# A hybrid encoder layer on eight cores: a convolution tap moved to VectorE, another order of tokens in PSUM, first norms and last block cut differently

## What is computed

```python
x = x + 0.5 * swiglu(rmsnorm(x, norm_ffn1[l]), w_ffn1_in[l], w_ffn1_out[l])
h = rmsnorm(x, norm_mix[l])
aq, ak, av, mq, mk, mv, mo, mif, cq, gts = jnp.split(h @ w_in[l], split_pts, axis=-1)
# mixer A: 24 heads of 64, groups (window, dilation) = (128,1), (512,4), (2048,16)
aq = rope(rmsnorm(ah(aq), att_q_gain[l])) * (ATT_HEAD_DIM ** -0.5)
ak = rope(rmsnorm(ah(ak), att_k_gain[l]))
y_att = dilated_attention(aq, ak, ah(av)).astype(x.dtype)
# mixer B: bidirectional mLSTM, behind a centred depthwise convolution of width 5
mqk = jax.nn.silu(centred_dwconv(jnp.concatenate([mq, mk], axis=-1), ml_conv_w[l], ml_conv_b[l]))
...
# mixer C: cross-attention of 4 heads into 256 memory tokens
...
merged = (g[:, :, 0] * (y_att @ w_br_att[l]) + g[:, :, 1] * (y_ml @ w_br_ml[l])
          + g[:, :, 2] * (y_cx @ w_br_cx[l]))
x = x + merged @ w_out[l]
x = x + 0.5 * swiglu(rmsnorm(x, norm_ffn2[l]), w_ffn2_in[l], w_ffn2_out[l])
x = rmsnorm(x, norm_final[l])
```

## Time and profile before

| | |
|---|---|
| runs shown (us) | 3948.44, 4095.29, 4669.13; median 4095.29 |
| profiled execution | 3949.09 us |
| its span on the slowest core (core 6) | 3947.6 us; the eight cores 3931.2 to 3947.6 |
| granted TensorE clock, mean of the cores | 0.992 to 0.995 |
| TensorE matmul, weight load | 97%, 49% of the span; 23860 matmuls |
| VectorE, ScalarE, GpSimd | 44%, 37%, 26% |
| DMA, mean | 67 GB/s |

### The profile page before, as it was taken

How to read it: one execution, slowest core, us unless ns; L and a number is a source line. 1 busy time by engine, 2 the same in 40 slices (tenths; PEclk the granted TensorE clock), 3 DMA queues, 4 the chain that set the end, 5 groups by cost and what they waited for, 6 DMA issues and landing times.

```text
span 3947.6 us, 64651 instructions; the slowest of 8 cores (3931.2 to 3947.6 us)
## 1 busy us (share of the span) xinstructions
PE 3811.1 (97%) x23860; PEld 1932.7 (49%) x23860; DVE 1755.9 (44%) x2559; ACT 1444.7 (37%) x2389; POOL 1035.8 (26%) x1048
## 2 busy tenths in 40 slices
PE   6999999998999999999989999999889999999998
PEld 2444457644555444444434444666455544444443
DVE  3121425656884444121441214357578744432214
ACT  4101233477775222101331012345778842321012
POOL 3010124346771012000221002144367601110002
PEclk9999999999999999999999999999999999999999
DMA  6152332343345433222444213225233433332212
GB/s 139 23 80 32 90 65 52 76 87 67 61 87 100 76 71 50 40 36 39 111 109 58 38 26 107 54 55 108 55 71 72 101 70 76 70 51 39 38 23 89
DMA packets 252882, 265.74 MB, mean 67 GB/s; under 512 B 161440, under 2 KB 179104, under 8 KB 250272
## 3 DMA queue, kind: packets, MB, share of 16 engines
q0 software_dynamic: 65088, 127.04, 21.8%
q1 hardware_dynamic: 187488, 134.58, 12.6%
HBM read 318.31 MB, written 57.67 MB: 95 GB/s over the span
## 4 chain that ended last, share of the span: by engine, by line
PE 91%; DVE 3%; ACT 2%; issue 2%; POOL 1%; DMA 1%; SPq 0%; DVEq 0%; POOLq 0%; ACTq 0%
PE ps L467 91%; DVE arena L467 3%; ACT arena L467 2%; POOL arena L467 1%; DMA arena<-arena 0%; ACT L467 0%; SPq L467 0%; DMA arena<-x 0%; DMA arena<-scr_y 0%; DMA scr_y<-arena 0%; DVEq L466 0%; POOLq L484 0%; ACTq L466 0%; DVEq L484 0%; POOLq L466 0%
## 5 line engine op out<-in xcount | busy, mean ns | idle before, releaser
L467 PE MATMUL ps<-arena 128*128 128x512 bf16 (+5 forms) x23860 | 3811.1, 321 | 126.2 <-DVE arena L467 50.8
L467 PEld LDWEIGHTS ps<-arena 128*128 128x128 bf16 x23860 | 1932.7, 99 | 2004.4 <-issue 228.3
L467 ACT ACTIVATE arena<-ps 128x512 bf16<-128x512 f32 (+7 forms) x1346 | 820.3, 638 | 1745.1 <-PE ps L467 1722.4
L467 DVE TENSOR_TENSOR arena<-ps,arena 128x512 f32<-128x512 f32 (+4 forms) x936 | 714.3, 776 | 1486.4 <-PE ps L467 1403.1
L467 POOL TENSOR_TENSOR arena<-arena 128x512 f32<-128x512 bf16 (+4 forms) x592 | 792.4, 1352 | 802.1 <-DVE arena L467 375.4
L467 DVE SCALAR_TENSOR_TENSOR arena<-ps,arena 128x512 f32<-128x512 f32 (+2 forms) x488 | 343.3, 710 | 401.2 <-PE ps L467 352.3
L467 ACT ACTIVATE arena<-arena 128x512 f32<-128x512 f32 (+3 forms) x654 | 387.2, 608 | 288.8 <-DVE arena L467 259.5
L467 DVE TENSOR_TENSOR arena<-arena 128x512 bf16<-128x512 f32 (+5 forms) x428 | 341.0, 805 | 60.0 <-ACT arena L467 40.2
L467 ACT ACTIVATE arena<-ps,arena 128x512 f32<-128x512 f32 (+3 forms) x320 | 204.3, 657 | 389.2 <-PE ps L467 365.7
L467 DVE SCALAR_TENSOR_TENSOR arena<-arena 128x512 bf16<-128x512 f32 (+2 forms) x296 | 233.1, 853 | 70.7 <-ACT arena L467 66.0
L467 POOL DMA_DIRECT2D arena<-wst x120 | 68.0, 567 | 521.1 <-PE ps L467 520.4
(11 more groups left out here) (16 smaller groups left out, 32.3 us busy)
## 6 DMA issues: line engine op xcount, KB each, us to landing
arena<-wst POOLq DMA_DIRECT2D x120, 256.0 KB, 4.2
arena<-w1a POOLq DMA_DIRECT2D x88, 256.0 KB, 4.9
arena<-w2a POOLq DMA_DIRECT2D x88, 256.0 KB, 4.5
arena<-x SPq DMA_DIRECT2D x32, 512.0 KB, 7.7
scr_x<-arena SPq DMA_DIRECT2D x8, 2048.0 KB, 9.2
arena<-scr_x SPq DMA_DIRECT2D x32, 512.0 KB, 9.4
out<-arena SPq DMA_DIRECT2D x32, 512.0 KB, 2.8
scr_v<-arena SPq DMA_DIRECT2D x48, 256.0 KB, 3.0
```

Of the source, the lines that this page charges most:

```text
L467: ins = getattr(eng, rec.name)(**rec.kwargs)
```

## The change

Six edits in one:

1. `conv` leaves its fifth tap to DVE: four matmuls, then one multiply-add on DVE which reads the bank and `cb` and writes a float32 tile (`cvr`), from which SiLU reads. The diagonal matrices have four parts.
2. In the attention, PSUM holds a window's tokens in the order token mod 4. Group two then writes neighbouring columns, group three every fourth, and group one writes, and reads its q, in four runs. q of group one is stored by class in each block (a rearranged read in `sc` on POOL), the masks are permuted on the host, and the closing multiplication puts tokens back in order.
3. The matrix of ones is written by a memset on DVE; the rest of `cbf` is loaded later. The norms of the first two blocks (`direct`) take squares on ACT, DVE and POOL and eight matmuls, without pair sums.
4. The down projection and final norm of the very last block go in two halves of 256 tokens (`tail`).
5. Regions move: mLSTM's first buffers to the beginning of `RX`, `v_stage` behind them, cross-attention's elsewhere.
6. Banks and order: cross-attention's raw queries have one bank, the first pair's projection three, the last pair's scores three; the steps of cross-attention are written s4 to s1.

```diff
         S.dma(out=vecs, in_=vecs_d)
-        S.dma(out=cbf, in_=cbf_d, queue="pool")
+        S.dve.memset(ap=cbf[:, 1, :], constant=1.0)
...
+            if direct:
+                for kc in range(8):
+                    sq = nsq.next()[:, 0:n]
+                    xs_ = xT[:, tb, kc, c0:c0 + n]
+                    if kc % 4 < 2:
+                        S.act.activation(out=sq, in_=xs_, func=AF.Square)
+                    else:
+                        (S.dve if kc % 4 == 2 else S.pool).tensor_tensor(out=sq, in0=xs_, in1=xs_, op=ALU.mult)
+                    S.pe.matmul(out=o_, lhsT=ones_b, rhs=sq, start=(kc == 0), stop=(kc == 7))
...
+                        if tail and tb == 3:
+                            for c0 in (0, 256):
+                                for d in range(8):
+                                    outmm(w2all[d], d, tb, OB.next(), c0, 256)
+                                final_tb(nseq - 1, tb, c0, 256)
+                            continue
...
-            PR_, PC = Rot([0, 1]), Rot([2, 3])
+            PR_, PC = Rot([0]), Rot([2, 3])
...
-                PA = Rot([4, 5]) if p == 0 else Rot([4, 5, 3])
+                PA = Rot([4, 5, 1]) if p == 0 else Rot([4, 5, 3])
...
-                    if r == 1:
+                    if r == 1 and isq:
+                        o = by_class(dst[:, tb * 512:(tb + 1) * 512], 4)
+                        a, c = (t.rearrange("p (i c) -> p c i", c=4) for t in (t1, t2))
+                    elif r == 1:
                         o, a, c = dst[:, tb * 512:(tb + 1) * 512], t1, t2
...
+                SB2 = Rot([0, 1, 3]) if p == 3 else Rot([0, 1])
...
                             if g == 0:
-                                ka, qv, vt = k_[0][:, sl, kt * 128:(kt + 1) * 128], q_[0][:, qa:qa + n], kt
-                                of = lambda bk: ps[:, bk, qa % 512:qa % 512 + n]
+                                w0, t0 = qa // 512 * 512, qa % 512
+                                ka, vt = k_[0][:, sl, kt * 128:(kt + 1) * 128], kt
+                                qv = q_[0][:, w0:w0 + 512].rearrange("p (r i) -> p r i", r=4)[:, :, t0 // 4:(t0 + n) // 4]
+                                of = lambda bk: ps[:, bk, :].rearrange("p (r i) -> p r i", r=4)[:, :, t0 // 4:(t0 + n) // 4]
                             elif g == 1:
                                 ka = k_[1][:, sl, cls * 512 + kt * 128:cls * 512 + (kt + 1) * 128]
                                 qv, vt = q_[1][:, cls * 512 + qa:cls * 512 + qa + n], cls * 4 + kt
-                                of = lambda bk: ps[:, bk, :].rearrange("p (i r) -> p r i", r=4)[:, cls, qa % 128:qa % 128 + n]
+                                of = lambda bk: ps[:, bk, cls * 128 + qa % 128:cls * 128 + qa % 128 + n]
...
-                        S.dve.tensor_tensor(out=yt[a0:a0 + 64, :], in0=ps[a0:a0 + 64, bk, :], in1=r1[a0:a0 + 64, :], op=ALU.mult)
+                        S.dve.tensor_tensor(out=yt[a0:a0 + 64, :].rearrange("p (i r) -> p i r", r=4),
+                                            in0=ps[a0:a0 + 64, bk, :].rearrange("p (r i) -> p i r", r=4),
+                                            in1=r1[a0:a0 + 64, :].rearrange("p (r i) -> p i r", r=4), op=ALU.mult)
...
-            nx = regions((RX[0] + 24576, RX[1]))
+            nx = regions((RX[0], RX[0] + 13824))
+            nb0 = regions((RX[0] + 34304, RX[1]))
...
-                        for j in range(5):
+                        for j in range(4):
                             S.pe.matmul(out=bank(bk), lhsT=dg[:, j, :], rhs=cb[:, tb * 512 + j:tb * 512 + j + 512],
-                                        start=(j == 0), stop=(j == 4))
-                        S.act.activation(out=B["kT" if isk else "qT"][:, tb * 512:(tb + 1) * 512], in_=bank(bk), func=AF.Silu,
+                                        start=(j == 0), stop=(j == 4 - 1))
+                        src = bank(bk)
+                        for j in range(4, 5):
+                            cs = cvr.next()
+                            S.dve.scalar_tensor_tensor(out=cs, in0=cb[:, tb * 512 + j:tb * 512 + j + 512],
+                                                       scalar=vcol(V_CW + ch * 5 + j), in1=src, op0=ALU.mult, op1=ALU.add)
+                            src = cs
+                        S.act.activation(out=B["kT" if isk else "qT"][:, tb * 512:(tb + 1) * 512], in_=src, func=AF.Silu,
                                          bias=vcol(V_CB + ch), scale=1.0)
```

88 lines of the change are left out of this document (48 added, 40 removed).

## The result

| | before | changed |
|---|---|---|
| undisturbed executions (us) | 3948.44, 3947.75 | 3924.01, 3924.33, 3923.53 |
| profiled execution (us) | 3949.09 | 3924.01 |
| span, slowest core; all eight (us) | 3947.6; 3931.2 to 3947.6 | 3922.5; 3913.1 to 3922.5 |
| ratio, 95% interval | | 0.9939 [0.991, 0.9968] |

What follows compares the result with a forecast made beforehand. The prediction took PE (TensorE), busy 97%, as the bound. Its terms, -13.8 + 4 - 26.9 + 6 - 5 - 4 - 3 - 4 - 3.4, summed to -50.1 us from 3949.1, so 3899 us, range 3870 to 3935.

Steps and rivals of the forecast that it cites:

- What bounds the kernel now: Whole kernel: PE busy 97%, leading in the attention stretches too, so fewer PE columns count fully where PE never idles.
- PSUM order, -26.9: Attention, middle group's matmuls with P and V: neighbouring columns take 0.44 us per 896, not 0.86; 26.9 us less.
- What pays for the order, +6: Attention: strided POOL query additions (27 us) and DVE closing multiplications (25 us) cost 6 us net; bounds 0 and +27.
- Runs of group one, 0: Attention, first group: writing and reading four runs of 16, 48 or 64 columns costs nothing; upper bound +29.8 us.
- The first sentence that the prediction cites: PSUM writes: any non-contiguous pattern slows matmuls significantly; taken literally for the first group's runs, 29.8 us more.
- Group three, 0: Attention, third group: going from 16 apart to 4 apart changes nothing; bounds -3.8 and +2 us.
- Convolution, -13.8 + 4: mLSTM convolution: 64 matmuls fewer save 13.8 us; new waits for the bank cost 4, bounds 0 and +45.
- Seam, -4: Seam into the mixer: earlier-freed buffers cut PE's idle and half-pace time by 4 us; bounds 0 and -12.
- Banks and first copies, -4, -3: Attention start: 4 of 11.8 us waiting for k copies saved; last head pair: 3 us saved for both sequences.
- Start, -5: First two norms: shared squares and fewer POOL steps save 5 us; first projection before 19 us, stream before 33.
- Last block, -3.4: End of kernel: final norm in halves shortens the last DVE operations and steps ahead by 3.4 us; bounds -1.6 and -5.
- The third, 3919 at 0.11: Rival: half of PE's order gain and of the convolution gain become waits for DVE and POOL; 3919 us, chance 0.11.

Runs made afterwards that it cites:

- part 4: Changed kernel without the order token mod 4, third group's mask added on PE instead of multiplied on DVE: 3905.35 to 3913.55 us, mean span 3899.3.
- part 2: Changed kernel with closing multiplication plain, POOL's query addition plain, or both (results differ): mean spans 3913.9, 3906.6 and 3898.1 us.
- part 6: Changed kernel with ACT's Ln in token order: mean span 3910.4 us; with ACT's exponential also making the order, mask on DVE: 3889.8.
- the one with both prices away: Changed kernel with closing multiplication and POOL's query addition both side by side, hand-back to token order left out: 3901.15 to 3915.20 us, mean span 3898.1.

## Why the prediction was wrong, point by point

**What bounds the kernel now.** The failing step is "PE leads, and two engines are close behind" together with "Fewer PE columns are worth their full time wherever PE has no idle time". In the attention stretches PE's 232.55 of 240 counted as full. It was not, in the sense of the sum. PE there waits again and again for a result of DVE, which is late by DVE's own queue and by POOL, and work taken from PE came back in part as such waits. 13.8 us more of PE with less DVE cost nothing (part 4), and 22 us less of PE with nothing against it made the kernel 6 to 14 us faster (parts 2 and 6). Over the whole run of the changed kernel PE is busy 23 us less than before, and idle as long as before (133 us, means of six cores).

**PSUM order, -26.9.** Two faults in size. The stretches of 0.44 and 0.86 us hold 1024 columns (six matmuls of 64, 192, 256, 256, 192, 64; twelve of 64, 128, 64) and not 896. So the gain on PE is 57,344 / 1024 x 0.40 = 22.4 us. The count of 57,344 was right. By the same fault the upper bound for the runs should have been 26 and not 29.8. And of these 22.4 us only 5.6 (part 2) to 13.9 (part 6) reach the end.

**What pays for the order, +6.** Measured 19 to 21 us (part 2, at the same order of all queues); with the gain that does not arrive, this is the term that was mis-sized most. The single prices were right (1.041 us against 0.686 + 0.39; POOL's 2.1). The share that is felt was not: I had let a third be felt of 64 operations at 0.3 us, and the addition's delay of POOL reached PE by way of DVE's queue, at 11 us of swap waits. One effect was missing altogether: the mask products beside POOL, 160 x 0.133 = 21 us more of DVE than before.

**Runs of group one, 0.** Right: 0.44 us. The first sentence that the prediction cites from the Trainium skill (Advanced Engine Details and Errata, PSUM Cachelines), taken literally, falls for runs of 16 and more; for single steps it stands. **Group three, 0.** Right: 0.47 against 0.46 us.

**Convolution, -13.8 + 4.** The DVE operation measured 0.743 us as taken; the wait term should have been 8 to 11. By my matching of the matmuls, the two mLSTM stretches are only 1.7 and 0.3 us shorter than with the tap on PE, for 6.9 us less of PE's work in each. PE's waits ahead of the transposes that end the mLSTM grew from 0.5 and 0.3 us to 3.2 in each; the rest of the difference is not traced.

**Seam, -4.** Too small: with the tap back on PE the stretch is still 8.5 + 5.1 us shorter than before. PE's idle time in it fell by 5.8 and 2.2 us; the rest, which can also be work that moved over the stretch's ends, is not traced. The two errors cancel, which is why the row of the table looks right (-15.4 for -13.8).

**Banks and first copies, -4, -3.** -7.7 and, without the order, -3.3 twice in the last pair (56.7 and 56.2 us). Both are about twice what I took. PE's wait for the copies is gone, and in its place stands one of 1.9 us for v. The output projection behind has 2 us more to do in each sequence, because less of it was mixed into the last pair.

**Start, -5.** Measured -4.6, though PE's first projection came at 19.07 and its stream at 34.34, and not before 19 and 33. **Last block, -3.4.** Measured -1.6. The last rows of the changed kernel, start and end:

```profile
19.07 1.01 PE L467 MATMUL ps<-arena 128*128 128x512 bf16 x2 [2.68 <-DMA arena<-w1a]
...
34.34 10.92 PE L467 MATMUL ps<-arena 128*128 128x512 bf16 x35 [0.43 <-POOL arena L467]
...
3914.51 3.26 DVE L467 SCALAR_TENSOR_TENSOR arena<-arena 128x256 f32<-128x256 f32 x8 [2.92 <-ACT arena L467]
```

The last eight operations did shrink from 5.39 to 3.26 us; of the steps ahead little came.

**The rivals.** The third, 3919 at 0.11, is nearest to what happened. Waits for DVE are 75.6 us, over the 60 of the forecast and a little under the 80 that I had named for this rival. Its way was right and its sum was partly luck: it gave back half of 26.9 and half of the convolution's gain, where the order gave back all of its 22.4 and 13 more, and everything else won 37 for 29. Against it I had put "waits for DVE are only 50.8 us over the run", a figure of a kernel with more work on PE, which hides lateness that shows as waits once the work is gone. The measured 3924 lies within 3870 to 3935 by the width of that range, not by the mechanism.

**What stays open.** Against the kernel without the order, the one with both prices away has 10 us more of waits, 7 at the third group's mask and 4 at the swap matmul, with 3 less at the output bank. Why DVE is late for just these masks in one kernel and not in the other (14.2 and 4.2 us) is open: their queues have nearly the same order (136 of PE's places differ), and these masks take 1.04 us each in the one and 0.76 in the other. How much of it is the planner's order is open too.

## What to carry to other kernels

Where PE is 97% busy and another engine stands at over 80%, find out which engine's time is cheap before you spend one for another. Moving a little work between them, as in part 4, shows it. A saving on the leading engine counts only until the others' late results become its waits. When an operand must be reordered, let ACT do it as it reads PSUM, keep steps out of SBUF operands, and count what VectorE operations with two SBUF operands lose beside GpSimd work (here 0.42 us became 1.30). When you scale by a row, count its columns from the matmuls in it.

## What the runs showed of the hardware

- ACT reads PSUM with a step of 4 or of 128 words for nothing (546 ns for 448 columns and 591 for 512 on 64 partitions, as without it). DVE, over 64x512, reads PSUM 128 words apart for nothing (0.685 us), SBUF in fp32 128 words apart for +0.36, and writes bf16 every fourth element for +0.62.
- PE's output in four runs of 16 to 64 columns costs nothing. A bf16 moving operand costs nothing more in such runs, and 0.42 for 0.22 us at every fourth element.
- A DVE product of 128x512 in bf16 with both inputs in SBUF takes 0.42 us with no POOL arithmetic beside it (436 of 1280, none over 0.43), and 1.30 us in the mean with it.
- PE's clock: where the last pair begins, PE is busy 1.68 of 4 us, and the next 8 us stand at a granted clock of 0.50, the 1.2 GHz level. Idle time in the last pair can therefore cost a second time; how much of the 8 us it cost here is not separated.

```profile
1157.00:1161.00 4.00, 1.68 (x38) 1.25 (x37) 3.79 (x4) 3.49 (x7) 3.96 (x5) 0.87 0.79 143
1161.00:1169.00 8.00, 5.74 (x49) 4.07 (x50) 6.87 (x7) 2.32 (x5) 7.48 (x8) 0.50 0.67 156
```
